# A one-layer encoder kernel on one Trainium2 core: inputs also stored channel-major, the latents computed first, the convolution spread between the attention steps

## What is computed

```python
h = rmsnorm(x, g_mix)
u = h @ w_in                       # 256 + 128 + 32 + 2*512 = 1440 columns
y_mla  = mla_attention(u[:, :256], u[:, 256:384], u[:, 384:416], ...)   # 8 heads, block-causal
y_conv = conformer_conv(u[:, 416:], w_dw, ...)   # GLU, causal depthwise conv of width 31, LayerNorm, swish
x = x + concat([y_mla, y_conv]) @ w_out
x = x + memory_cross_attention(rmsnorm(x, g_xattn), rmsnorm(mem, g_mem), w_xq, w_xkv, w_xo)  # 4 heads, 256 memory tokens
x = x + moe_ffn(rmsnorm(x, g_ffn), ...)          # top 4 of 32 experts, each 1024 -> 2048 -> 1024
return rmsnorm(x, g_final)
```

## Time and profile before

| | |
|---|---|
| median of 3 runs | 1207.36 us |
| the profiled execution | 1207.0 us |
| its span in the profile | 1205.3 us |
| PE busy | 1141.0 us, 95% of the span |
| DVE, ACT, POOL busy | 330.5, 237.0, 86.2 us |
| DMA from HBM | 434.61 MB |
| first expert matmul (L1486) starts | 286.69 us |

### The profile page before, as it was taken

The page is one execution under the profiler, slowest core; times in us unless marked ns, Lnnn a source line. Parts: engine busy times, 40 slices in busy tenths (PEclk is TensorE's granted clock), DMA queues, the critical chain, the costliest instruction groups (busy, mean ns, idle before and its releaser), DMA issues.

```text
span 1205.3 us, 16320 instructions
## 1 busy us (share of the span) xinstructions
PE 1141.0 (95%) x5306; PEld 500.5 (42%) x5307; DVE 330.5 (27%) x859; ACT 237.0 (20%) x453; POOL 86.2 (7%) x204
## 2 busy tenths in 40 slices
PE   6969999998999999999999999999999999999996
PEld 5747548752333333334333333343333333333332
DVE  1388731323222211112222111222211111111113
ACT  2213121311121121111211211112112111111112
POOL 1098000002000000000000000000000000000000
PEclk9979999998999999999999999999999999999999
DMA  8230733736999999999999999999999999999994
GB/s 352 105 148 1 279 140 140 284 152 279 425 427 427 430 428 427 427 429 428 430 428 428 427 431 428 427 428 430 429 426 428 430 429 426 427 430 430 427 426 175
DMA packets 37461, 435.99 MB, mean 362 GB/s; under 512 B 4947, under 2 KB 5118, under 8 KB 12862
## 3 DMA queue, kind: packets, MB, share of 16 engines
q1 hardware_dynamic: 37438, 435.67, 85.9%
HBM read 434.61 MB, written 1.05 MB: 361 GB/s over the span
## 4 chain that ended last, share of the span: by engine, by line
PE 76%; DMA 18%; DVE 4%; ACT 2%; issue 0%; SPq 0%; ACTq 0%; DVEq 0%
PE bank L1486 28%; DMA ring<-in_w_up_dram 17%; PE bank L1501 16%; PE bank L1440 5%; PE total L1453 4%; PE bank L1365 2%; PE bank L1192 2%; PE bank L1214 2%; PE bank L1447 1%; DVE ring L907 1%; PE bank L1522 1%; PE bank L1205 1%; PE total L1404 1%; PE bank L1404 1%; PE total L1184 1%; PE bank L1526 1%
## 5 line engine op out<-in xcount | busy, mean ns | idle before, releaser
L1486 PE MATMUL bank<-ring,buf_m 128*64 128x512 f32 x2112 | 464.4, 595 | 21.7 <-DMA ring<-in_w_up_dram 20.0
L1486 PEld LDWEIGHTS bank<-ring,buf_m 128*64 128x64 f32 x2112 | 150.2, 137 | 329.8 <-issue 289.4
L1501 PE MATMUL bank<-ring,buf_m 128*64 128x512 f32 x1056 | 239.5, 595 | 0.0
L1115 DVE COPY buf_f<-bank 128x512 f32<-128x512 f32 x33 | 22.8, 692 | 562.9 <-PE bank L1486 562.9
L1501 PEld LDWEIGHTS bank<-ring,buf_m 128*64 128x64 f32 x1056 | 72.8, 136 | 137.5 <-issue 129.2
L763 ACT ACTIVATE buf_f<-bank 128x512 f32<-128x512 f32 x33 | 19.7, 597 | 375.0 <-PE bank L1486 375.0
L1453 PE MATMUL total<-buf_m,wr_sb 64*128 64x512 f32 x272 | 67.6, 615 | 0.8 <-ACT buf_m L775 0.8
L1440 PE MATMUL bank<-buf_k,buf_v 128*64 128x512 f32 x272 | 67.5, 618 | 0.7 <-DVE buf_v L1066 0.7
L543 POOL TENSOR_TENSOR buf_v<-table,buf_v 128x4 f32<-128x4 f32 x33 | 6.6, 199 | 778.6 <-DVE buf_v L1103 778.2
L1121 DVE TENSOR_TENSOR buf_f<-bank,buf_v 128x512 f32<-128x512 f32 x66 | 45.4, 688 | 59.5 <-PE bank L1522 59.5
L760 ACT ACT_TABLE_LOAD x33 | 42.3, 1283 | 33.7 <-issue 33.7
(11 more groups left out here) (327 smaller groups left out, 919.4 us busy)
## 6 DMA issues: line engine op xcount, KB each, us to landing
ring<-in_w_up_dram SPq DMA_DIRECT2D x128, 2048.0 KB, 29.8
ring<-in_w_down_dram SPq DMA_DIRECT2D x64, 2048.0 KB, 29.6
ring<-in_w_in_dram SPq DMA_DIRECT2D x4, 1440.0 KB, 11.1
ring<-in_w_xkv_dram SPq DMA_DIRECT2D x2, 2048.0 KB, 23.9
ring<-in_w_xkv_dram SPq DMA_DIRECT2D x1, 4096.0 KB, 14.4
ring<-in_w_out_dram SPq DMA_DIRECT2D x1, 4096.0 KB, 14.4
ring<-in_w_xq_dram SPq DMA_DIRECT2D x2, 2048.0 KB, 21.3
ring<-in_w_xo_dram SPq DMA_DIRECT2D x1, 4096.0 KB, 12.9
```

The lines of the kernel that those rows point to most:

```text
L1486: ins = t_.matmul(banks[c][h * 64:(h + 1) * 64, :], xg[:, k, :], w[:, h * FF + c * BANK:h * FF + (c + 1) * BANK], start=k == 0, stop=k == ...
L1501: ins = t_.matmul(banks[2][h * 64:(h + 1) * 64, :], actT[:, f, :], group(slot_of(at))[:, part * D + h * BANK:part * D + (h + 1) * BANK], s ...
```

## The change

The host now also hands over x and memory channel-major (`x_t`, `mem_t`), all per-channel vectors and taps in one array (`by_channel`), and w_in reordered: first the latents' columns, then each convolution block's 128 value and 128 gate columns. The jobs `vec`, `hT` and `mT` and their transposes go. In their place:

- `gained`: `hT` is x times its gain, not yet normalised. The latents' projection reads it, and the row scale 1/rms is applied when `u0` (ACT) and `u1` (DVE) are drained.
- `rx`, `rm`: a matrix of ones times a diagonal of the row scales gives the scales along the free axis. DVE multiplies `hT` by `rx` to `hTn` (for the convolution) and `mem_t` by gain and `rm` to `mT`.
- PE computes the latents first; each convolution block is a job of its own (`conv_job`): `cv0` before `cqT`, `cv1` before q, `cv2` after the values, `cv3` after `qT`. All four `xk` jobs come after the scores.
- GpSimd takes block 0 and starts when `cv0` is drained. DVE does blocks 1 to 3: 14 and 11 taps of block 1 alone, then pieces of two blocks in turn, and the last 56 instructions together between the softmax and the draining of `o`.
- q's rms scale is applied when ACT drains q, not before `cqT`.

The core of the diff:

```diff
-    jobs = [("vec", "v", "v")]
-    jobs += [(f"hT{i}", "v", "v") for i in range(4)]
-    jobs += [(f"u{t}", "v", "v") for t in range(2)]
-    jobs += [(f"cv{c}", "a", "v") for c in range(4)]
-    jobs += [(f"mT{i}", "a", "a") for i in range(4)]
...
             def conv_taps(*pieces):
+                for w, c in [(w, c) for at in range(max(len(ws) for c, ws in pieces))
+                             for c, ws in pieces for w in ws[at:at + 1]]:
...
+                        dve.wait_ge(conv_step, conv_at[c])
+                        ins = v.scalar_tensor_tensor(acc[:, c, :], src, wt, acc[:, c, :], ALU.mult, ALU.add)
...
+            dve.wait_ge(loaded["memT"], 16)
+            wait_full(dve, "rm")
+            for k in range(KT):
+                ins = v.scalar_tensor_tensor(mT[:, k, :], mT[:, k, :], gm_sb[:, k:k + 1], bank_of("rm")[:, 0:T],
+                                             ALU.mult, ALU.mult)
...
+            gated(1)
+            conv_taps((1, taps_of[:14]))
...
-            conv_taps(range(10, 13))
+            conv_taps((1, taps_of[14:25]))
+            gated(2)
+            conv_taps((1, taps_of[25:]), (2, taps_of[:6]))
+            gated(3)
...
-            conv_taps(range(13, 24))
+            conv_taps((2, taps_of[6:]), (3, taps_of))
...
-            conv_taps(range(24, TAPS))
             dve.wait_ge(conv_step, conv_n[0])
...
             for k in range(KT):
+                if k == 6:
+                    pe.wait_ge(diag_ready, TT)
+                    end("rx", t_.matmul(begin("rx")[:, 0:T], ones[:, :], part("PT1")[:, 0:T], start=True, stop=True))
+                pe.wait_ge(h_ready, k // 2 + 1)
+                pe.wait_ge(loaded[f"wu{k // 2}"], 16)
...
-            wait_drained(pe, "mT3")
-            key_job(0)
-            key_job(1)
-            pe.wait_ge(cq_ready, 4)
+            conv_job(0)
+            wait_drained(pe, "u0")
+            wait_drained(pe, "u1")
```

More of the change, by code:

```diff
@@ L18 @@
 CT = CONV // P
-CONV_V = 3
 TOK_COLS = Q_LORA + KV_LORA + ROPE
@@ L38, in trunk_jobs @@
 def trunk_jobs():
-    jobs = [("vec", "v", "v")]
-    jobs += [(f"hT{i}", "v", "v") for i in range(4)]
-    jobs += [(f"u{t}", "v", "v") for t in range(2)]
-    jobs += [(f"cv{c}", "a", "v") for c in range(4)]
-    jobs += [(f"mT{i}", "a", "a") for i in range(4)]
-    jobs += [(f"xk{i}", "a", "a") for i in range(2)]
-    jobs += [("cqT", "v", "v"), ("ckvT", "v", "v"), ("krT", "a", "a")]
+    jobs = [("u0", "a", "a"), ("rx", "v", "v"), ("u1", "v", "v"), ("cv0", "a", "v")]
+    jobs += [("cqT", "v", "v"), ("ckvT", "v", "v"), ("krT", "a", "a"), ("rm", "v", "v"), ("cv1", "a", "v")]
     jobs += [(f"q{t}{h}", "a", "a") for t in range(2) for h in range(2)]
@@ L50, in trunk_jobs @@
     jobs += [(f"v{t}", "a", "a") for t in range(2)]
+    jobs += [("cv2", "a", "v")]
     jobs += [(f"qT{i}", "a", "a") for i in range(4)]
+    jobs += [("cv3", "a", "v")]
     jobs += [(f"s0{i}", "v", "v") for i in range(2)]
     jobs += [(f"s1{i}", "v", "v") for i in range(4)]
-    jobs += [(f"xk{i}", "a", "a") for i in range(2, 4)]
+    jobs += [(f"xk{i}", "a", "a") for i in range(4)]
     jobs += [(f"pT0{i}", "a", "a") for i in range(2)]
@@ L368, in _ @@
[L368 to L374, removed]
@@ L914, in _ @@
+            gated(0)
             wait_full(dve, "cqT")
@@ L1187, in _, with conv_job @@
                         end(f"u{t}", ins)
-                for c in range(CT):
-                    for g in range(2):
-                        at = TOK_COLS + g * CONV + c * P
-                        ins = t_.matmul(cb[c][:, g * T:(g + 1) * T], w_in_sb[:, k, at:at + P], hT[:, k, :],
-                                        start=first and g == 0, stop=last and g == 1)
-                    if last:
-                        end(f"cv{c}", ins)
-            pe.wait_ge(memn_ready, TT)
-            transposes("mT", memn)
+            def conv_job(c):
+                b = begin(f"cv{c}")
+                pe.wait_ge(loaded[f"wc{c}"], 16)
+                for k in range(KT):
+                    if c == 0 and k < 6:
+                        pe.wait_ge(hn_ready, k // 2 + 1)
+                    if c == 0 and k == 6:
+                        wait_drained(pe, "rx")
+                    for g in range(2):
+                        ins = t_.matmul(b[:, g * T:(g + 1) * T], wc_sb[:, c, k, g * P:(g + 1) * P], hTn[:, k, :],
+                                        start=k == 0 and g == 0, stop=k == KT - 1 and g == 1)
+                end(f"cv{c}", ins)
@@ L1235, in _ @@
             end("krT", ins)
+            pe.wait_ge(diag_ready, 2 * TT)
+            end("rm", t_.matmul(begin("rm")[:, 0:T], ones[:, :], part("PT1")[:, T:2 * T], start=True, stop=True))
+            conv_job(1)
             wait_drained(pe, "cqT")
```

289 lines of the change are left out of this document (152 added, 137 removed).

## The result

| | before | after |
|---|---|---|
| median | 1207.17 us (4 runs, 1206.74 to 1211.65) | 1179.85 us (4 runs, 1179.44 to 1180.29) |
| span of the profiled execution | 1205.3 us | 1178.1 us |
| PE, DVE, POOL busy | 1141.0, 330.5, 86.2 us | 1132.7, 332.1, 86.7 us |
| last key job ends (start + length) | 121.26 us | 94.25 us |
| first expert matmul starts | 286.69 us | 259.68 us |

The changed kernel is faster: the ratio of the times is 0.9766, with a 95% interval of 0.9742 to 0.9789.

A forecast was written before the change was run, and what follows sets the result against it. PE bounds the trunk and sets off the expert weight stream. Gains of 7.5, 11.9, about 3.3, 2.5 and 0.8 make 26.0 us; 1207.0 - 26.0 = 1181.0, plus 0.4 gives 1181.4, range 1179 to 1183.5 (0.62).

The forecast's parts named there:

- The bound: Expert loop: PE starting expert 0 sets off the weight stream; 918.6 us from there stay unchanged, so trunk gains arrive in full.
- The start: Trunk's beginning: PE starts at 5.0 us, runs 6 us at half pace, and the latents end at 19.9.
- first loads late: Rival, chance 0.12: first loads stay at 214 GB/s, latents end at 23.9 instead of 19.9 us; total 1185.4.
- PE's walk: Changed trunk followed on PE: last key job ends at 95.3 us instead of 121.3, a gain of 26.0.
- The wait of 11.9 us: After the latents' transposes PE waits for DVE, which drains `cqT` behind 30 taps; removing this gains 11.9 us.
- Its clock: Half-rate PE clock after the 11.9 us wait, slowing q; its removal gains about 3.3 us.
- The earlier start: Beginning of PE's work in the trunk: starting earlier gains 7.5 us.
- The wait before the keys: PE's wait for ACT before the key jobs, 2.46 us; its removal gains 2.5 us.
- DVE keeps up: Hand-overs before `qT` and `oT`: at 0.72 us per lone tap DVE is ready about one microsecond ahead of PE.
- The rival that took the ceiling: Chance 0.17: lone taps take 0.94 us, one per GpSimd instruction; DVE becomes the bound, 4.1 us lost, 1185.5.
- Hidden: Rival, chance 0.02: the weight stream runs ahead by itself and hides the trunk's gain; total 1207.
- cold: Rival, chance 0.02: PE stays at 1.2 GHz, work from 11 to 67.4 us doubles, +56 us; total 1237.

The follow-up runs named there:

- experiment 2: Changed kernel with 28 extra lone taps on DVE, results thrown away, ahead of draining cqT, putting the old wait back: 1194.43 us.
- experiment 4: Changed kernel with two of the four key jobs moved from behind the scores to before them: 1189.06 us.
- experiment 8: Changed kernel with 24 small identity matmuls into unused PSUM banks in PE's five short pauses of the routing: 1177.34 us.
- experiment 5: Changed kernel with the two halves of x loaded before the per-channel array and the first pair of x_t and weights: 1182.62 us.
- experiment 1: Kernel before, with only DVE's order changed: cqT and ckvT drained behind 12 taps instead of 30: 1202.1 us, ratio 0.9947.
- experiment 3: Changed kernel without GpSimd's taps 1 to 30 of block 0, so its output is not the layer's: 1204.75 us.
- experiment 9: Changed kernel with the routing pauses filled and twelve small identity matmuls at PE's start, running until the first real matmul: 1181.62 us, in two clusters.
- experiment 10: Kernel of experiment 9 with the second half of DVE's angles put behind the diagonals: 1176.4 us, ratio to the kernel before 0.9749.
- experiment 7: Changed kernel with nine small identity matmuls at PE's start and its wait for GpSimd's constants moved to `rx`: 1179.55 us.

## Why the prediction was right, step by step

**The bound.** Right. The stretch from the first expert matmul is 918.4 us, forecast 918.6. In experiments 2 and 4 the first expert matmul is 13.1 and 8.1 us later and the span 13.2 and 8.1 us longer, so what reaches the experts reaches the end.

**The start.** Two errors that cancelled, by luck. Forecast: PE starts at 5.0 and is at half pace for 6 us. It starts at 6.29, and the records are 0.69 us apart only until about 10. The start was late because I applied 394 GB/s, from two halves of x, to the first small pieces; the stream made 150 GB/s from 2 to 4 us and 308 from 4 to 6, DVE had x_t at 5.19 and PE its weights at 6.29, where the forecast had both in at 4.8. The length at half pace was taken from one pause; it was 3 us (experiment 8) to 5 us (experiment 5) over these runs. The latents ended at 19.86, forecast 19.9. Of the rival "first loads late" this is the true part: 1.3 us, not four.

**PE's walk.** Forecast 28.4 for `cv1`, 40.5 for the end of q, 67.4 for the end of the scores, 95.3 for the keys. Measured: 28.08, 40.24, 66.46 and 94.09. The sum was 1.2 us too long, of which 0.35 are `qT`, 0.4 the scores and 0.3 the keys. Those lengths were taken as the printed lengths of groups, and a group's last record overlaps the next group. The 121.3 of before is such a printed end too, so the forecast of 26.0 answers to 121.26 - 94.25 = 27.0. With the 0.2 of the last stretch it is 27.2, and 1207.0 - 27.2 gives 1179.8, the time of the profiled execution within 0.2.

**The gain's parts.** The wait of 11.9 us is confirmed by putting it back (experiment 2) and, at the place, by removing it in the kernel before (experiment 1). Its clock was forecast at 3.3. From q's start to the next group it is 8.33 us before and 5.26 after, so 3.1, and 2.0 in experiment 2. The earlier start gave 12.56 - 6.29 = 6.3 us and not 7.5; that a start passes through is shown by experiment 5. The wait before the keys gave its 2.5. What is left of the 27.0 is 3.3 us, forecast 0.8: here the split of the sum was wrong, and its errors nearly cancel. The forecast had taken 6 us of half pace off it, and that lasts about 4 us in both kernels. This rest and the 2.5 were read from the timelines; no run isolates them.

**DVE keeps up.** Right, with more to spare than forecast: 2.2 and 2.8 us in place of about one. A lone tap beside GpSimd costs 0.68 to 0.69 us; I took 0.72, with a floor of 0.53 and a ceiling of 0.94. Undisturbed it is 0.51 (experiment 3). The rival that took the ceiling had rested on one tap for each GpSimd instruction. At this time GpSimd's additions start at 38.30 and 40.30, so a product and an addition take 2.0 us, and three lone taps fit in that, as three taps in turn did in 1.88 before. (Rows 10 show only GpSimd's side of this; the trace of before has DVE's tap at 72.53, next to the addition at 72.47.) The Trainium skill ("SBUF — State Buffer", section "Who interferes with whom") calls the ports that the two engines share an exclusive lock, and says of DVE's two-port modes that the loser blocks for the whole instruction. Carried over to these taps that would have given two in the 2.0 us, not three. The traces agree that the two engines contend (0.68 us a tap against 0.51), and not that an instruction waits for a whole one.

**The other rivals.** "Hidden" and "cold" did not happen. That PE could be cold at odd times was closer to the truth than I gave it: it cost 3.4 us in experiment 1, and in the routing it costs the kernel before and the changed one alike (the first expert's 64 records take 15.28 and 15.43 us, 13.95 with fillers).

## What to carry to other kernels

Put the drain that the bounding engine waits for ahead of the other engine's filler work, and check each hand-over by the time in hand: here the order alone was worth 10.4 us at the keys in the old layout, but only 5 us at the end, as the next wait (`oT`) and a lower clock took the rest. Before an engine is given a share to relieve another, price it by what the other one loses in pace: GpSimd's 31 taps took 31 instructions from DVE and gave its taps 2.9 us, and the whole of DVE 1.1. Short pauses of PE in a chain of small steps can cost more than their length, and fillers into an unused PSUM bank brought 2.8 us of that back here.

## What the runs showed of the hardware

- With PE cold, small matmuls raise its pace as well as large ones: after 3.6 to 4.5 us of fillers at 0.21 us a record they go at 0.11 (experiments 9 and 10), and the work behind them starts at full pace. With a pause of 0.72 us behind 4.2 us of fillers the work started at half pace (experiment 7). During this start the profile shows the granted clock as 1.00, although the records are twice as far apart; only their distance tells.
- The clock can be granted at one half while PE is busy without a gap: from 262 to 268 us in experiment 1, 244 to 248 in experiment 9. It is in the profiles of experiments 2 and 4 as well. In all four it falls at the router, in or just behind its 32 short records (32 columns), and the 8 transposes that follow take 6.33, 5.38, 5.38 and 5.19 us in experiments 1, 9, 2 and 4, instead of 3.68 in the kernels before and after, where the same matmuls stand. It need not cost time: from the router's first record to the first expert's it is 17.8 us in experiment 2 and 17.7 in 4, against 18.9 in the kernels before and after, as the gather behind the pauses then runs at full pace (1.94 us instead of 3.47 in the changed kernel). What sets it off stays open, and so does whether it makes the clusters of 3 to 4 us in the times of experiments 1 and 9: one execution of each was profiled.
- The first pieces of a stream are slow: 150 GB/s from 2 to 4 us and 308 from 4 to 6 in the changed kernel, 414 from 8 to 10.
- The stream of weights can stand still while PE is busy, and the time is not made up: 0 GB/s from 300 to 315 us and 25 us more in the end (experiment 3). The reading that an additional block of the first expert does it is an inference from SP's rows.
